# Products whose results nobody reads, in TensorE's waits in both routers and ahead of the transposes of the S5 output

## What is computed

```python
def _hmoe(h, w_group, b_group, w_expert, b_expert, w_gate, w_up, w_down):
    g_logits = xf @ w_group + b_group            # 520 x 4
    g_sel = argmax(g_logits); g_w = softmax(g_logits)[g_sel]
    e_in = (xf @ w_expert + b_expert)[group g_sel]
    top_v, top_i = top_k(e_in, 2); top_w = softmax(top_v) * g_w
    y = sum over the experts of (silu(x w_gate) * (x w_up) * top_w) w_down

# layer 1, between the S5 scan and its router
ag = gelu(y) @ w_glu
x = x + ag[:, :1024] * sigmoid(ag[:, 1024:])
x = x + _hmoe(rmsnorm(x), ...)
```

## Time and profile before

| | us |
|---|---|
| median of 3 runs | 1189.48 |
| lowest and highest | 1187.64, 1191.68 |
| the profiled execution | 1186.47 |
| its span | 1184.6 |
| PE busy | 987.3 (83%) |
| PEld, the weight loads of PE | 601.8 (51%) |
| DVE, POOL, ACT busy | 414.2, 331.2, 164.8 |
| chain that ended last | PE 54%, DMA 28%, DVE 8%, POOL 4% |

### The profile page before, as it was taken

How to read it: one execution, slowest core, us unless ns; L and a number is a source line. 1 busy time by engine, 2 the same in 40 slices (tenths; PEclk the granted TensorE clock), 3 DMA queues, 4 the chain that set the end, 5 groups by cost and what they waited for, 6 DMA issues and landing times.

```text
span 1184.6 us, 15841 instructions
## 1 busy us (share of the span) xinstructions
PE 987.3 (83%) x5780; PEld 601.8 (51%) x5780; DVE 414.2 (35%) x935; ACT 164.8 (14%) x304; POOL 331.2 (28%) x548
## 2 busy tenths in 40 slices
PE   4999999899688888788883539799996999787787
PEld 3888878444544444444423527444545555444442
DVE  3300055766542222212242892012365332222124
ACT  3201020132200000000122101410442000000012
POOL 0070000277366666666419200000001112111100
PEclk9999989899599999988995659799995999999998
DMA  7126630540789999999927272903017899999972
GB/s 247 36 71 218 234 113 20 216 169 37 265 333 422 418 421 416 406 384 397 358 59 101 36 108 82 399 27 142 36 30 305 347 421 422 424 424 427 420 294 87
DMA packets 53379, 289.37 MB, mean 244 GB/s; under 512 B 11787, under 2 KB 21771, under 8 KB 34599
## 3 DMA queue, kind: packets, MB, share of 16 engines
q1 hardware_dynamic: 38759, 264.69, 57.3%
q0 software_dynamic: 8928, 16.49, 3.7%
q10 hardware_dynamic: 5632, 7.41, 2.8%
HBM read 267.59 MB, written 35.06 MB: 255 GB/s over the span
## 4 chain that ended last, share of the span: by engine, by line
PE 54%; DMA 28%; DVE 8%; POOL 4%; ACT 2%; issue 2%; SPq 2%; DVEq 0%; ACTq 0%; POOLq 0%
DMA arena<-in_w_gu 19%; PE ps L681 12%; PE ps L930 10%; PE ps L808 7%; DMA arena<-in_w_down 7%; PE ps L1077 5%; POOL arena L2026 4%; PE ps L976 3%; DVE arena L1423 3%; PE ps L920 3%; PE ps L982 2%; PE ps L1052 2%; PE ps L1056 2%; PE ps L859 2%; PE ps L838 2%
## 5 line engine op out<-in xcount | busy, mean ns | idle before, releaser
L930 PE MATMUL ps<-arena 128*64 128x256 f32 x2048 | 247.4, 398 | 63.5 <-DMA arena<-in_w_gu 61.9
L930 PEld LDWEIGHTS ps<-arena 128*64 128x64 f32 x2048 | 152.3, 143 | 159.8 <-DMA arena<-in_w_gu 50.1
L2092 POOL TENSOR_TENSOR arena<-arena 128x256 f32<-128x256 f32 (+3 forms) x192 | 132.6, 691 | 40.7 <-POOL arena L2092 40.3
L681 PE MATMUL ps<-arena 128*128 128x260 f32 x640 | 141.4, 383 | 0.0
L920 PE MATMUL ps<-arena 128*64 128x512 f32 x512 | 121.9, 619 | 13.3 <-DMA arena<-in_w_down 12.8
L681 PEld LDWEIGHTS ps<-arena 128*128 128x128 f32 x640 | 121.1, 190 | 18.8 <-issue 0.4
L2026 POOL TENSOR_TENSOR arena<-arena 128x32 f32<-128x32 f32 (+5 forms) x165 | 83.4, 506 | 157.9 <-ACTq L1237 142.5
L808 PE MATMUL ps<-arena 128*128 128x512 f32 x256 | 118.8, 616 | 2.5 <-DVE arena L1569 2.4
L1793 DVE TENSOR_TENSOR arena<-arena,ps 128x128 f32<-128x128 f32 x64 | 18.4, 288 | 274.3 <-ACT arena L1326 274.3
L1326 ACT ACTIVATE arena<-ps 128x128 f32<-128x128 f32 x64 | 17.8, 278 | 494.0 <-PE ps L930 494.0
L2123 POOL COPY idx_now<-idx_list 128x1 int32 (+1 forms) x32 | 6.2, 194 | 275.8 <-DVEq L1708 261.3
(11 more groups left out here) (219 smaller groups left out, 1001.2 us busy)
## 6 DMA issues: line engine op xcount, KB each, us to landing
arena<-in_w_gu SPq DMA_DIRECT2D x64, 2048.0 KB, 13.2
arena<-in_w_down SPq DMA_DIRECT2D x64, 1024.0 KB, 14.4
arena<-in_w_in SPq DMA_DIRECT2D x10, 1024.0 KB, 6.0
scratch_yd<-arena SPq DMA_DIRECT2D x2, 4160.0 KB, 16.4
arena<-scratch_yd SPq DMA_DIRECT2D x16, 512.0 KB, 7.6
arena<-in_w_out SPq DMA_DIRECT2D x1, 4096.0 KB, 12.8
scratch_hd<-arena ACTq DMA_DIRECT2D x8, 512.0 KB
arena<-in_w_glu SPq DMA_DIRECT2D x2, 2048.0 KB, 7.7
```

The costliest lines, as they stand in the source:

```text
L681: mm = pe.matmul(o[:, b, 0:HALF], w[:, kc, (n % 2) * P:(n % 2 + 1) * P], HT[:, kc, b * HALF:(b + 1) * HALF], start=kc == 0, stop=kc == KC - 1)
L930: mm = pe.matmul(ps[CAP * f:CAP * f + CAP, 2 + s, 0:256], XT[l][:, kc, CAP * s:CAP * s + CAP], WGU[l][i][s][:, kc, 256 * f:256 * f + 256], ...
L2092: g_.tensor_tensor(o, x, y, f).then_inc(sem("matrix_steps"), 1)
```

## The change

A helper `keep_busy(out, n)` issues n products of the 128x128 identity with 256 columns of tile 0 of `X`, each with start and stop, into a PSUM area that nobody reads before it is written again. No semaphore is counted for them. It is called

- in both routers ahead of `transpose(4)` (7 products in layer 0, 11 in layer 1), ahead of `logits(4)` (5), ahead of `position(4)` (17), behind it (4), ahead of the second lists (14) and behind them (8): 55 products in layer 0, 59 in layer 1;
- once in the S5 part, 12 products between the last `y` products and the first transposes of `yT`.

The calls stand ahead of the waits of the steps that follow them. Nothing else is changed, and no other engine's program is.

```diff
+            def keep_busy(out, n):
+
+                for _ in range(n):
+                    pe.matmul(out[:, 0:256], ident, X[:, 0, 0:256], start=True, stop=True)
...
                 main(4, [(transpose, 2)], [(logits, 2), (transpose, 3)], [(logits, 3), (position, 1), (position, 2)])
+                early, late = main_slot(l, 1)[:, 1, :], main_slot(l, 0)[:, 0, :]
+                keep_busy(early, 11 if l else 7)
                 transpose(4)
                 position(3)
+                keep_busy(late, 5)
                 logits(4)
+                keep_busy(late, 17)
                 position(4)
+                keep_busy(late, 4)
                 pe.wait_ge(sem("tr_copied"), 5 * l + 5)
                 for k in range(5):
                     pe.wait_ge(sem("ranked"), 5 * l + k + 1)
...
                 done(pe.matmul(total_slot(l), ones, both, start=True, stop=True), "total", 0)
+                keep_busy(late, 14)
                 pe.wait_ge(sem("weighted"), l + 1)
                 for k in range(5):
                     mm = list_part(1, k)
                 mm.then_inc(sem(f"list_done_{l}"), 1)
+                keep_busy(late, 8)
...
                 full(mm)
+            ring.wait_free(pe, "yT", 0)
+            keep_busy(slot("yT", 0)[:, 0, :], 12)
             for kc in range(KC):
                 ring.wait_emptied(pe, "y", kc)
```

## The result

| | median us | lowest to highest | ratio to before, 95% interval |
|---|---|---|---|
| before | 1188.56 | 1186.02 to 1191.68 (6 runs) | |
| changed | 1201.66 | 1198.18 to 1206.85 (6 runs) | 1.011 (1.0076 to 1.0144) |

The changed kernel is slower by 13.1 us, in the direction of the forecast (+8.5 on the profiled execution, 1197.0 as the time). The time lies 0.7 us above the range's upper end, 1201.0.

What follows compares the result with a forecast made beforehand. The prediction took each DMA-filled expert stage to hang on its first load, behind the router tail's PE, DVE, ACT chain. Terms 2.0 + 3.4 + 3.1 = +8.5 us gave 1195.0 on the profiled run, set at 1197.0; range 1192.5 to 1201.0.

Steps and rivals of the forecast that it cites:

- The price of a product: Each added 256-column product makes two rows and costs 0.43 us on PE at full clock, twice that at half.
- The chain in the routers: Router tails: fills outlast the waits, delaying each step; first expert loads later by 2.0 us (layer 0) and 3.4 (layer 1).
- Full clock "taken as given": Router 0: PE has no gap over 0.5 us from 294 to 326, so full clock was assumed.
- the third rival: Routers: the clock falls under the fills, next fill at 0.86 us a product until it rises; +12 to +14, 1202; 8%.
- The S5 part: S5 output: 12 products, 5.16 us, ahead of the transposes delay the first GELU; +3.1 us, GLU still starting at half clock.
- The two thirds of the way: Time set at 1197.0, between 1195.0 (from the profiled run) and 1198.0 (from the median), as slower runs may have longer half-clock stretches.
- one such term: The range reaches 4 us up from the forecast, for one fill at half clock.
- The first rival: Fills fit their waits because a product costs 0.22 us: sum -5.5 us, 1184; 6%.
- The second rival: S5 output: work ahead of the transposes holds the clock up to the GLU; +5 or less, 1193, within noise; 8%.

Runs made afterwards that it cites:

- `gelu`: Changed kernel, with ACT doing a one-column GELU ahead of its wait for the first transposes, so the table loads under the fill; 1.0112, 1200.1 us.
- `narrow`: Changed kernel with 128 instead of 256 columns in each added product, counts unchanged; 1.0002 of the kernel before, 1187.98 us.
- `routers`: Changed kernel without the 12 products ahead of the transposes of yT; the 55 and 59 in the routers stay; 1.0069, 1197.0 us.
- `gelu2`: The kernel with the GELU table loaded under the fill, timed again beside the changed kernel; 1.0123, 1203.59 us, against 1203.93 for the changed kernel.
- `again`: The changed kernel run once more, with nothing altered; 1.0128 of the kernel before, 1203.93 us.
- `mix`: Changed kernel with 128-column products, except a last fill of 11 products of 256 in both routers, none in the S5 part; 0.9956, 1183.17 us.
- `mix15`: Changed kernel with 128-column products, last fill of 256 columns: 11 products in layer 0, 15 in layer 1; none in S5; 0.9969, 1185.09 us.
- `inlists`: Changed kernel with the same number of products, but one behind each of the first four parts of both lists; 1.0113, 1200.9 us.
- `hd`: Changed kernel, 128-column fills, last one 4 products of 256, none in S5; some down weights issued only after the normed rows land; 1.0005, 1187.39 us.
- `hd_alone`: Kernel before, no added product, with only some down weights issued after the normed rows have landed; 1.0016, 1189.36 us.

## Why the prediction was right and wrong

- **The price of a product** was right, and it decided: 0.43 us, from the two rows a product; 34 rows took 7.4 us in the trace, 7.31 in the sum. With half the columns the loss is gone.
- **The chain in the routers** was right step by step up to the lists: 1.1, 2.2, 3.8, 5.1 forecast, 1.21, 2.43, 4.03, 5.33 measured. Small things (0.436 instead of 0.43 us a product, 2.37 instead of 2.3 for a list, 0.23 for the product of the totals, 3.9 instead of 3.7 from the gate-up products to the load) add up: a router without a fall of the clock costs 2.5 and 4.05 instead of 2.0 and 3.4, 1.2 us in all. DVE's read of the first list is 2.8 later by the terms of the sum, not 2.7, and was 3.1 later (316.27 in the changed kernel); nothing waited for it.
- **Full clock "taken as given"** was wrong. It rested on PE having no gap over 0.5 us. In the traces of this kernel PE was busy and the clock fell, once in one of the two routers, under the 14 products: 1.7 us. That is the third rival, which had 8%, in the mildest form: it gave up to 5.5 us for it. Its time, 1202, lies next to the measured 1201.66 by luck: the fall is 1.7 of the missing 4.6 us, and the table load and the small things, which it did not have, make up the rest.
- **The S5 part** was 4.6 instead of 3.1. The failed step is "the first GELU at 743.39, behind ACT's own copies and table load": I took the load as part of the cover. Written as part of the GELU instruction it stands behind the instruction's wait for the transposes. Before, they had come by the time of the load (742.10), so the row could not show which of the two it followed. `gelu` shows 1.2 us of the 1.5; another 0.1 is the fill, 5.28 instead of 5.16.
- **The two thirds of the way** from the profiled execution to the median, for half clock that the fills would save, had no ground. On the median of all six runs the sum gives 1188.56 + 8.5 = 1197.1, so it did no harm. What is missing is 1.2 + 1.7 + 1.5 = 4.4 of the 4.6 us by which 13.1 exceeds 8.5. I had widened the range for one such term, and three came together.
- **The first rival** had the mechanism that `narrow` shows, with the price that the kernel doesn't have. Its time was too good (-5.5 forecast, -1.8 in the trace, none in the median): the S5 part cost 2.1 instead of 0.5, most of it the table load of 1.28, and the clock did not stay up to the gate-up products.
- **The second rival** did not occur: with 5.3 us of fill ahead of the transposes, the clock was at half when the GLU began.

## What to carry to other kernels

Price a filler by the rows it makes in the trace, not by the calls: a float32 product is two rows and each wait must be longer than the fill that stands ahead of it, or the fill itself becomes the chain. Raising the clock pays where the work behind it is long (here the first pair's gate-up products, 2.9 us shorter in router 0 and 1.6 in router 1) and where something else, here a gather behind a DMA write, ends last anyway; ahead of work that has no wait it only costs. The best sizes found here gave 0.4%. Look also at what was hidden by the thing that you move: a table load inside an instruction waits with it.

## What the runs showed of the hardware

- TensorE's clock fell with the engine busy all the time, after 2.6 us of products of 32 columns between dense ones. Of the five traces with the full fills, four had it in router 0 (the changed kernel, `routers`, `gelu`, `gelu2`) and one in router 1 (`again`). In `narrow`, `mix` and `mix15`, whose fills are half as long, it fell in router 0 within 1.4 us of the end of a list as well, under the fill behind it (near 317.0, 309.3 and 310.5). What decides which list it follows, and why the other routers had none there, is open. It also fell in places that no kernel changes: eight rows of layer 1's `main` took 5.40 us instead of 3.70 in `gelu2` (891.11), `inlists` (887.84) and `hd_alone` (876.74), with no wait of PE ahead of them.
- A write of 0.5 MB issued at 302.9 landed near 315 in `narrow`, with 6 MB of weight loads issued from 298.7 on ahead of it; with 4 MB ahead of it, it took 11.8 us (`hd`) and 10.9 (`hd_alone`) to POOL's start, against 12.1. A gather of the first tokens took 3.8 us to land in router 0 of `narrow`, and 5.0 to 7.2 with 2 MB of weights issued just ahead of it (`hd`, `hd_alone`).
- The same stage took the same time to 0.02 us in different executions (GLU +4.58 in three, first load of router 1 +4.05 in four), while six executions of one kernel spread over 6 to 12 us. Differences of one or two microseconds can be read from a stage, and not from medians.
